# Expert weights in 2 MB transfers: two ring slots and one semaphore for each

## What is computed

```
D_MODEL = D_EXPERT = 1024; N_EXPERTS = 32; TOP_K = 4

logits = (h @ w_router + b_router).astype(F32)
top_logit, top_idx = lax.top_k(logits, TOP_K)
top_p = jax.nn.softmax(top_logit, axis=-1)
...
def expert_block(args):
    tok, p, e = args
    xb = h_pad[tok]
    gu = xb @ w_gu[e] + b_gu[e]                     # w_gu (32, 1024, 2048)
    glu = jnp.minimum(gu[:, :D_EXPERT], SWIGLU_LIMIT)
    lin = jnp.clip(gu[:, D_EXPERT:], -SWIGLU_LIMIT, SWIGLU_LIMIT)
    act = glu * jax.nn.sigmoid(SWIGLU_ALPHA * glu) * (lin + 1.0)
    return (act @ w_down[e] + b_down[e]) * p[:, None].astype(h.dtype)   # w_down (32, 1024, 1024)
```

## Time and profile before

| | |
|---|---|
| runs | 2170.11, 2170.84, 2176.09 us |
| median | 2170.84 us |
| profiled execution, its own time | 2173.72 us |
| its span, first to last instruction | 2171.1 us |
| mean granted clock of TensorE | 0.963 of 2.4 GHz |
| TensorE busy | 1936.4 us, 89% |
| VectorE, ScalarE busy | 622.1 and 434.6 us |
| read from memory | 555.26 MB, 261 GB/s over the span |

### The profile page before, as it was taken

How to read it: one execution, slowest core, us unless ns; L and a number is a source line. 1 busy time by engine, 2 the same in 40 slices (tenths; PEclk the granted TensorE clock), 3 DMA queues, 4 the chain that set the end, 5 groups by cost and what they waited for, 6 DMA issues and landing times. The chain is left out here.

```text
span 2171.1 us, 24938 instructions
## 1 busy us (share of the span) xinstructions
PE 1936.4 (89%) x9338; PEld 1049.2 (48%) x9340; DVE 622.1 (29%) x1362; ACT 434.6 (20%) x855; POOL 67.3 (3%) x86
## 2 busy tenths in 40 slices
PE   5999797998989979999898888989989888979997
PEld 2436353886878543333333333233333245657774
DVE  2376346245520121111111111111111123442223
ACT  2122550326231011111111110111111022411011
POOL 1000310100000000000000000000000000000000
PEclk9999898798999989999999999999999999989998
DMA  9443336214374469999999999999999872034442
GB/s 348 144 167 137 131 98 145 94 55 143 93 282 164 161 248 418 418 418 417 417 417 418 418 417 419 418 419 418 416 418 417 336 267 78 1 118 153 162 148 87
DMA packets 150651, 566.73 MB, mean 261 GB/s; under 512 B 35872, under 2 KB 43808, under 8 KB 112736
## 3 DMA queue, kind: packets, MB, share of 16 engines
q1 hardware_dynamic: 150592, 565.92, 67.2%
HBM read 555.26 MB, written 10.62 MB: 261 GB/s over the span
## 5 line engine op out<-in xcount | busy, mean ns | idle before, releaser
L2006 PE MATMUL expert_gb<-expert_ring,hT 128*64 128x512 f32 x1024 | 270.4, 607 | 69.6 <-DMA expert_ring<-in_w_gu 68.1
L2006 PE MATMUL expert_lb<-expert_ring,hT 128*64 128x512 f32 x1024 | 262.8, 592 | 0.0
L1911 DVE TENSOR_SCALAR hT<-expert_gb 128x512 f32<-128x512 f32 x32 | 22.1, 692 | 717.0 <-PE expert_lb L2006 717.0
L2054 PE MATMUL expert_yb<-expert_ring,hT 128*64 128x512 f32 x512 | 222.7, 592 | 1.5 <-DMA expert_ring<-in_w_down 1.4
L2054 PE MATMUL expert_yb<-expert_ring,h2T 128*64 128x512 f32 x512 | 222.8, 592 | 0.0
L2006 PEld LDWEIGHTS expert_gb<-expert_ring,hT 128*64 128x64 f32 x1024 | 59.4, 135 | 250.2 <-DMA expert_ring<-in_w_gu 200.5
L446 PE MATMUL mix_in_pj<-hT,mix_in_pj_ring 128*128 128x512 f32 (+1 forms) x384 | 147.1, 542 | 4.0 <-DVE hT L567 4.0
L2006 PEld LDWEIGHTS expert_lb<-expert_ring,hT 128*64 128x64 f32 x1024 | 72.8, 137 | 147.0 <-issue 147.0
L2711 PE MATMUL ffn_pu<-ffn_hT,ffn_wu 128*128 128x256 f32 x640 | 141.4, 379 | 0.0
L2054 PEld LDWEIGHTS expert_yb<-expert_ring,hT 128*64 128x64 f32 x512 | 69.9, 137 | 143.3 <-issue 140.5
L2711 PEld LDWEIGHTS ffn_pu<-ffn_hT,ffn_wu 128*128 128x128 f32 x640 | 121.6, 190 | 25.1 <-issue 9.6
(11 more groups left out here) (474 smaller groups left out, 2288.1 us busy)
## 6 DMA issues: line engine op xcount, KB each, us to landing
expert_ring<-in_w_gu SPq DMA_DIRECT2D x256, 1024.0 KB, 19.7
expert_ring<-in_w_down SPq DMA_DIRECT2D x128, 1024.0 KB, 20.7
fill_w<-in_w_fill SPq DMA_DIRECT2D x48, 512.0 KB, 3.7
mix_in_wm<-in_w_mod SPq DMA_DIRECT2D x11, 2048.0 KB, 9.1
ffn_wu<-in_w_up_units SPq DMA_DIRECT2D x22, 1024.0 KB, 6.2
mix_in_pj_ring<-in_w_in_units SPq DMA_DIRECT2D x12, 1024.0 KB, 4.8
ffn_wd<-in_w_down SPq DMA_DIRECT2D x22, 512.0 KB, 3.4
expert_ring<-in_w_in SPq DMA_DIRECT2D x4, 2048.0 KB, 11.4
```

The costliest lines, as they stand in the source:

```text
L1911: v.tensor_scalar(glu, gb[j][:], LIMIT, None, ALU.min).then_inc(s_glu, 1)
L2006: m = pe.matmul(b[halves[h], :], xT[:, k, x], ring[:, z, c0 + 512 * h:c0 + 512 * h + 512], start=False, stop=(k == KT - 1))
L2054: m = pe.matmul(yb[h][halves[j], :], hidT[j][:, c, hh * SLOTS:(hh + 1) * SLOTS], ring[:, z, a * F + 512 * h:a * F + 512 * h + 512], start= ...
```

## The change

Units are loaded two at a time. `load_expert_units` takes an even u and fills slots z and z + 1 with one transfer of 2 MB, which raises one semaphore, `S.landed[z // 2]`; six semaphores are left of twelve. For `w_gu` each partition gets the rows of two neighbouring units, 128 rows apart. For `w_down` each partition gets four rows of one expert; so units 16 and 17 now belong to the first expert, 18 and 19 to the second, 20 and 21 to the first, 22 and 23 to the second, and TensorE finds unit n of expert j at 16 + 4 (n // 2) + 2 j + n % 2. SP waits until both units that held the two slots are used. TensorE raises `s_used` as before in the up projection, and in the down projection by 2 behind the second unit of a pair (n = 1 and n = 3).

```diff
-def load_expert_unit(sp, A, S, pair, u):
+def load_expert_units(sp, A, S, pair, u):
     z = u % EXPERT_RING
-    dst = S.ring[:, z, :]
+    dst = S.ring[:, z:z + 2, :]
     if u < 2 * KT:
         e, n = pair * 2 + u // KT, u % KT
-        src = A.w_gu[bass.ds(e, 1), n * P:(n + 1) * P, :].rearrange("e p n -> (e p) n")
+        src = A.w_gu[bass.ds(e, 1), n * P:(n + 2) * P, :].rearrange("e (a p) n -> p (e a) n", p=P)
     else:
-        e, n = pair * 2 + u % 2, (u - 2 * KT) // 2
-        src = A.w_down[bass.ds(e, 1), 2 * n * P:2 * (n + 1) * P, :].rearrange("e (a p) n -> p (e a) n", p=P)
-        dst = dst.rearrange("p (a n) -> p a n", a=2)
-    sp.dma_start(dst, src).then_inc(S.landed[z], 16)
+        e, n = pair * 2 + (u // 2) % 2, (u - 2 * KT) // 4
+        src = A.w_down[bass.ds(e, 1), 4 * n * P:4 * (n + 1) * P, :].rearrange("e (a p) n -> p (e a) n", p=P)
+        dst = dst.rearrange("p z (a n) -> p (z a) n", a=2)
+    sp.dma_start(dst, src).then_inc(S.landed[z // 2], 16)
...
                     with sp.Fori(0, PAIRS - 1) as i:
-                        for u in range(RING, PER):
-                            sp.wait_ge(s_used, (p * PAIRS + i) * PER + (u + 1))
-                            load_expert_unit(sp, A, S, i, u)
+                        for u in range(RING, PER, 2):
+                            sp.wait_ge(s_used, (p * PAIRS + i) * PER + (u + 2))
+                            load_expert_units(sp, A, S, i, u)
...
-                            pe.wait_ge(landed[z], it * 32 + 16 * (u // RING + 1))
+                            pe.wait_ge(landed[z // 2], it * 32 + 16 * (u // RING + 1))
...
                     for n in range(4):
                         for j in range(2):
-                            u = 2 * KT + 2 * n + j
-                            pe.wait_ge(landed[u % RING], it * 32 + 16 * (u // RING + 1))
+                            u = 2 * KT + 4 * (n // 2) + 2 * j + n % 2
+                            pe.wait_ge(landed[u % RING // 2], it * 32 + 16 * (u // RING + 1))
                         for a in range(2):
...
-                                    if a == 1 and h == 1:
-                                        m.then_inc(s_used, 1)
+                                    if a == 1 and h == 1 and n % 2 == 1:
+                                        m.then_inc(s_used, 2)
```

More of the change, by code:

```diff
@@ L1566, in _ @@
                 sp.wait_ge(s_pa, 2)
-                for n in range(8, 12):
-                    load_expert_unit(sp, A, S, 0, n)
+                for n in range(8, 12, 2):
+                    load_expert_units(sp, A, S, 0, n)
                 sp.wait_ge(s_y, 1)
-                for n in range(4):
-                    load_expert_unit(sp, A, S, 0, n)
+                for n in range(0, 4, 2):
+                    load_expert_units(sp, A, S, 0, n)
                 sp.wait_ge(s_t, 4)
-                for n in range(4, 8):
-                    load_expert_unit(sp, A, S, 0, n)
+                for n in range(4, 8, 2):
+                    load_expert_units(sp, A, S, 0, n)
                 sp.wait_ge(s_tab, 128)
@@ L1844, in body @@
                     with sp.Fori(0, PAIRS - 1) as i:
-                        for u in range(RING, PER):
-                            sp.wait_ge(s_used, (p * PAIRS + i) * PER + (u + 1))
-                            load_expert_unit(sp, A, S, i, u)
[L1848 to L1853, removed]
+                        for u in range(RING, PER, 2):
+                            sp.wait_ge(s_used, (p * PAIRS + i) * PER + (u + 2))
+                            load_expert_units(sp, A, S, i, u)
+                        for u in range(0, RING, 2):
+                            sp.wait_ge(s_used, (p * PAIRS + i) * PER + (PER + u + 2))
+                            load_expert_units(sp, A, S, i + 1, u)
+                    for u in range(RING, PER, 2):
+                        sp.wait_ge(s_used, p * (PAIRS * PER) + ((PAIRS - 1) * PER + u + 2))
+                        load_expert_units(sp, A, S, PAIRS - 1, u)
                     with sp.If(count > p * SLOTS + SLOTS):
-                        for u in range(RING):
-                            sp.wait_ge(s_used, p * (PAIRS * PER) + ((PAIRS - 1) * PER + PER + u + 1))
-                            load_expert_unit(sp, A, S, 0, u)
+                        for u in range(0, RING, 2):
+                            sp.wait_ge(s_used, p * (PAIRS * PER) + ((PAIRS - 1) * PER + PER + u + 2))
+                            load_expert_units(sp, A, S, 0, u)
                 count = sp.value_load(S.count[0:1, 0:1], min_val=0, max_val=L)
@@ L2820, in build @@
             S.count = mix.sb("count", [P, 1], I32)
-            S.ring, S.landed = mix.sb("expert_ring", [P, EXPERT_RING, 2 * D]), mix.sems("expert_landed", EXPERT_RING)
+            S.ring, S.landed = mix.sb("expert_ring", [P, EXPERT_RING, 2 * D]), mix.sems("expert_landed", EXPERT_RING // 2)
             S.pick = S.fill.w[:].rearrange("p a k n -> p (a k n)")[0:3 * NE]
```

2 lines of the change are left out of this document (1 added, 1 removed).

## The result

| | before | after |
|---|---|---|
| median of 8 runs | 2170.48 us | 2179.52 us |
| lowest to highest | 2169.38 to 2176.09 | 2175.65 to 2181.10 |
| profiled execution, its own time | 2173.72 us | 2178.96 us |
| its span | 2171.1 us | 2176.9 us |
| TensorE busy, mean clock | 1936.4 us, 0.963 | 1927.7 us, 0.960 |

The ratio is 1.0032, 95% interval 1.002 to 1.0044: the kernel is slower by some 7 us (the medians alone lie 9 us apart). Measured once more beside other runs of before, it was 1.0040 (1.0024 to 1.0055).

What follows compares the result with a forecast made beforehand. It took the expert stage to be bound by a never-stopping DMA stream that TensorE follows. Terms 1.72 + 3.44 + 0.8 - 1.7 = +4.3 us on the median of 2170.84 gave 2175.1 us, range 2169 to 2186.

Steps and rivals of the forecast that it cites:

- the hidden steady state: Expert stage after its start: TensorE catches the stream at the third pair, 6.6 us of queue cover remain; cost nothing.
- my own case: Whole kernel: the summed terms, +4.3 us, with a span of 2174.3 to 2178.5 us; chance 78%.
- the rival on hops: w_gu transfers: alternating rows 1 MB apart cost 4.7 ns a hop, 9.2 us on top, 2184 us; chance 12%.
- first refill waits for two units: Stage start: first refill waits for units 0 and 1, so the whole stream lies 1.72 us later.
- queue short of work in the first down projection: First pair of experts: slots given back at 833.3, no gap by 0.4 us, at worst about a microsecond.
- completions saved: Expert stream: 186 transfers fewer, each saving a completion packet per engine at 9.4 ns, 1.7 us saved.
- one more n step behind the last landing: Stage end: n = 2 and n = 3 both stand behind the last w_down landing, plus 3.44 us.
- half clock there: Stage end: 3.4 us of TensorE idle probably brings a half-clock stretch, 0 to 1.5 us, taken as 0.8.
- the part of the latency that follows the bytes: First pair of experts: latency by which the queue ran empty earlier than 834.3, or 836.0 with the later stream; no size given.
- signs of being wrong: Next profile: w_gu window not at 421 GB/s, DMA share below 1.0 inside the stage, or steady-state TensorE at half clock.
- dry queue: Slots of the first down pair: cover 7.6 us less, a microsecond a pair of experts, 15 us, 2190; chance 3%.
- faster by dearer completions: Expert stream: a completion weighs 0.075 us, so 186 fewer save 14.0 us, 2162.8 us; chance 7%.

Runs made afterwards that it cites:

- waits one unit later: The kernel before, with 1 MB transfers, each of SP's waits in the expert stage asking for one unit more to be used: ratio to before 1.0000.
- half transfers: The kernel before, each w_down unit brought by two transfers of 0.5 MB, same packets, 128 transfers more: ratio to before 1.0004.
- TensorE kept busy: The changed kernel with matmuls into an unused bank during TensorE's last wait: ratio to before 1.0040 with six matmuls, 1.0027 with three.

## Why the prediction was right, and where its terms were off

I had forecast 2175.1 us, within 2169 to 2186, and it became 2179.5. The direction, the two ends and the hidden steady state stand; the sum was too small, by terms that I can now name. That the range held was in part luck: 2179.5 lies above the 2174.3 to 2178.5 that my own case allowed, and it is in the range only because that was stretched for the rival on hops, which the runs refuted. I had also given 0.64 to a change too small to be seen, and both measurements have their whole interval above 1.

| term | forecast | measured | shown by |
|---|---|---|---|
| first refill waits for two units | +1.72 | +1.7 | the marks; waits one unit later |
| stream behind the refill | 0 | +0.1 | 1.8 us of bytes missing in the first 45 us, where the refill is 1.7 later |
| queue short of work in the first down projection | 0, at worst 1 | +0.8 | 403 for 420 GB/s; only w_down in pairs |
| completions saved | -1.7 | 0 to -0.3 | half transfers; 60.23 against 60.24 us a pair |
| one more n step behind the last landing | +3.44 | +3.4 | 8.4 against 4.9 us |
| half clock there | +0.8, at most 1.5 | +1.7 | TensorE kept busy |
| sum | +4.3 | +7.4 to +7.7 | the marks themselves give +7.8, 952.8 against 945.0 |

*The step that failed most* is "I take 9.4, since the DMA share is full and every packet's time shows in the pace". Eight completions more for each engine in a pair of experts should have made 0.08 us by it, and the half transfers show 60.24 us as before. A share above 1 says that packets overlap; that a completion does so wholly is my reading of this. I had the bound "nothing" beside it and took the wrong end. The price of 9.4 ns for each further row, from 2.56 against 2.485 us, was carried over to a packet of another kind.

*The gap in the queue*: "No gap, by 0.4 us" failed, though its times held: the pair was asked for at 831.9 us, which is 833.3 in before's time as forecast, and it landed 7.8 us later, 0.1 us from 836.0 + 4.97. But these are landings. The text names "the part of the latency that follows the bytes" and takes nothing off for it, and the bytes fell short while the last transfer had yet to land. The DMA share of 0.98 in those 10 us is one of the signs of being wrong that the prediction named. And the reasoning took the start and the gap for two terms. They are one: the stream can't be ahead of the slots that the first down projection gives back, so what an earlier start gains, the gap takes. A pair given back only behind n = 1 puts the last landing 2.3 to 2.7 us off at either start.

*The end* was right in place and in size: first two n steps ready at the landing (0.18 us of waiting, the forecast had 0.3), then 3.03 us idle (forecast 3.4), then two steps. The clock fell as one of the rows of before had let expect; I halved its price for uncertainty, and it came whole, in both profiles of the changed kernel. With waits of like length having gone either way, that it came at all was not certain. The bound of 1.5 us was read from matmuls of 128 columns; here it was 1.7.

*The steady state* held: pairs 4.98 us apart (forecast 4.97), no wait at n = 2, no dry queue. The shortest time from issue to landing there is 13.9 us for 2 MB.

*The rivals*: faster by dearer completions, refuted by half transfers. Slower by hops, refuted by w_gu in pairs (60.25 us a pair of experts). The dry queue came at its one weak place and nowhere else. The fixed 2.0 us in the Trainium skill, "DMA: Bandwidth & Descriptors", on the anatomy of one DMA, are given there for transfers that GpSimd issues, which the prediction left out; those here are SP's. By its two terms, an estimate, a lone 1 MB transfer takes 4.4 us, and 4.8 were measured. The stream it doesn't describe: 192 transfers fewer saved at most 0.3 us.

## What to carry to other kernels

Where the queue is never empty, the size of a transfer was free from 0.5 to 2 MB here, and only its latency is left: every wait for a larger piece costs one piece at the start, one at the end, and once more where the queue is at its thinnest. Before making transfers larger, look whether the gap that they should remove is in the trace at all; a DMA share of 1.02 says that it isn't. And with a stream that bounds a stage, count what stands before its first refill and behind its last landing, for everything else is hidden.

## What the runs showed of the hardware that I had not expected

- A completion packet costs a full stream nothing that these rows show: 24, 12 and 32 transfers in a pair of experts took 60.24, 60.23 and 60.24 us.
- After an idle time of 3.03 us TensorE's granted clock fell to 0.50, not at once but 1.4 us after work had begun again, for some 3 us; 3.06 us did the same in the second profile. The waits of 1.3 to 1.4 us in the steady state never did so. In between, the length does not tell: 1.87, 1.98, 2.27 and 2.42 us did so once each and 2.16 did not; the wait of 2.3 us in the first middle part did so in eleven profiles of twelve; and the 2.99 us ahead of the first up projection did so in one profile of ten.
- The same code met the slow stretch at different places from one execution to the next: the first up units took 1.92 us for four matmuls in one, 1.03 in the others. Since the stream hangs on the first refill, such a stretch there costs the whole kernel 2.4 us, where in the middle of the stage it would cost nothing.
